# Dense products of three gated stages in three f32r passes, with the delta output's norms moved one stage on

## What is computed

```python
z = h @ w_in[l]                       # split into the inputs of four mixers
o_a = hgrn2_mixer(a_q, a_f, a_i, a_g, lower_bounds[l], hgrn_norm_g[l])
o_b = gla_mixer(b_q, b_k, b_v, b_code, b_g, gla_w_gk2[l], gla_b_gk[l], gla_norm_g[l])
o_c = mla_mixer(c_q, c_kv, c_kr, ...)
o_d = gdn_mixer(d_q, d_k, d_v, d_beta, d_a, d_z, ...)     # gated delta rule
mix = concatenate([o_a, o_b, o_c, o_d]) @ w_out[l]
x = x + rms_norm(mix, post_mix_g[l])
```

## Time and profile before

| | us |
|---|---|
| median of 3 runs | 2296.11 (2295.84 to 2297.59) |
| the profiled execution, its own time | 2292.07 |
| its span in the profile | 2290.3 |
| PE busy | 2169.8 |
| DVE busy | 1208.1 |
| ACT busy | 898.2 |
| POOL busy | 45.6 |

### The profile page before, as it was taken

How to read it: one execution, slowest core, us unless ns; L and a number is a source line. 1 busy time by engine, 2 the same in 40 slices (tenths; PEclk the granted TensorE clock), 3 DMA queues, 4 the chain that set the end, 5 groups by cost and what they waited for, 6 DMA issues and landing times. The chain is left out here.

```text
span 2290.3 us, 35396 instructions
## 1 busy us (share of the span) xinstructions
PE 2169.8 (95%) x14540; PEld 1555.1 (68%) x14540; DVE 1208.1 (53%) x2075; ACT 898.2 (39%) x1611; POOL 45.6 (2%) x36
## 2 busy tenths in 40 slices
PE   7999999899999999989998999998999988999998
PEld 5784454588888777744446888886877566887546
DVE  5553344676662285543546666524537774444554
ACT  5423234433333354233344333333346553323462
POOL 2000001000000020000010000000000000000000
PEclk9999999999999999999999999999999999999999
DMA  5201110122222221011112222222221102222001
GB/s 199 74 3 46 48 55 32 63 92 97 106 92 92 92 74 56 22 38 56 38 38 80 104 92 92 102 82 97 97 90 56 38 19 92 93 92 85 26 1 37
DMA packets 23920, 159.79 MB, mean 70 GB/s; under 512 B 3024, under 2 KB 3664, under 8 KB 4944
## 3 DMA queue, kind: packets, MB, share of 16 engines
q1 hardware_dynamic: 23760, 157.53, 19.3%
HBM read 155.43 MB, written 2.10 MB: 69 GB/s over the span
## 5 line engine op out<-in xcount | busy, mean ns | idle before, releaser
L673 DVE TENSOR_TENSOR arena_r<-ring,arena_r 128x512 fp32r<-128x512 f32 x448 | 313.1, 706 | 453.7 <-ACT arena_r L664 450.9
L664 ACT ACTIVATE arena_r<-ring 128x512 fp32r<-128x512 f32 x448 | 278.3, 629 | 597.8 <-PE banks L714 566.4
L712 PE MATMUL banks<-oT_r,arena_r 128*128 128x512 f32 x1104 | 449.5, 407 | 13.0 <-DVE arena_r L673 9.0
L714 PE MATMUL banks<-oT_r,arena_r 128*128 128x512 f32 x1104 | 432.4, 392 | 0.0
L713 PE MATMUL banks<-hT_r,arena_r 128*128 128x512 f32 x928 | 363.6, 392 | 0.0
L713 PE MATMUL banks<-arena_r,arena_r 128*128 128x512 f32 x704 | 276.3, 392 | 0.0
L712 PEld LDWEIGHTS banks<-oT_r,arena_r 128*128 128x128 f32 x1104 | 208.8, 189 | 71.4 <-DVE arena_r L944 11.8
L712 PE MATMUL banks<-arena_r,arena_r 128*128 128x512 f32 x592 | 240.3, 406 | 15.2 <-DVE arena_r L704 10.9
L714 PEld LDWEIGHTS banks<-oT_r,arena_r 128*128 128x128 f32 x1104 | 208.5, 189 | 44.5
L714 PE MATMUL banks<-arena_r,arena_r 128*128 128x512 f32 x592 | 232.6, 393 | 0.0
L713 PEld LDWEIGHTS banks<-hT_r,arena_r 128*128 128x128 f32 x928 | 175.8, 189 | 41.6 <-issue 7.2
(11 more groups left out here) (387 smaller groups left out, 2927.7 us busy)
## 6 DMA issues: line engine op xcount, KB each, us to landing
ring<-weights SPq DMA_DIRECT2D x142, 1024.0 KB, 4.7
xT<-x_features SPq DMA_DIRECT2D x2, 1024.0 KB, 6.2
arena<-memory SPq DMA_DIRECT2D x2, 1024.0 KB, 4.9
y_features<-xT SPq DMA_DIRECT2D x8, 256.0 KB, 2.0
const<-constants SPq DMA_DIRECT2D x1, 1088.0 KB, 15.7
const<-constants SPq DMA_DIRECT2D x1, 512.0 KB, 16.4
arena<-positions SPq DMA_DIRECT2D x1, 256.0 KB, 2.7
small<-small_vectors SPq DMA_DIRECT2D x2, 68.5 KB, 6.4
```

The source lines that it names most:

```text
L664: act.activation(hi, self.stream.block(b, n), ACT.Copy).then_inc(self.chip.sem("hi_ready"), 1)
L673: vec.tensor_tensor(lo[:, 0:n * P], self.stream.block(b, n), hi[:, 0:n * P].bitcast(F32), ALU.subtract).then_inc(self.chip.sem("lo_ready"), 1)
L712: pe.matmul(out, w_hi, hi, start=k == 0, stop=False)
L714: ins = pe.matmul(out, w_lo, hi, start=False, stop=k == nk - 1)
```

## The change

1. In `Meanwhile.steps`, units from `first_split` on are made by `split_product_steps`, three f32r passes a block, instead of `product_steps`. `GLA_WHOLE = (1, 0, 2)` units of each gated stage stay whole: of 32, 40 and 32 blocks 24, 40 and 24 are split, 88 a layer, 176 in two layers.
2. ScalarE and VectorE make the parts. First gated stage: eight row tiles of `chip.h` and six weight chunks of four blocks. The second uses the same row parts and makes ten chunks. The third: four row tiles (`chip.o` 0, 1, 6, 7) and six chunks. ScalarE's copies of rows and of the first chunks stand before the copy of the log decays into `LF_HI`, which is now line 1770 and signals `silu_ready`.
3. The norms of the delta output leave the delta stage. Its squares and gate products stay there; the two norm matmuls, the Ln and Exp and the two products come in the first gated stage, late (`left = 2`).
4. The blocks between the steps are given by a table, `GLA_RUNS`.
5. SP's loads in these stages wait for low parts of the ring's slot and for the whole units (`whole`). Of five empty blocks in the weights' layout three move ahead of `outad`, so its chunks start on a multiple of four.

```diff
     def steps(self, pe):
         for u in range(self.u0, self.u1):
-            for k in product_steps(self.chip, pe, self.stream, u, self.rhs):
+            if u < self.first_split:
+                walk = product_steps(self.chip, pe, self.stream, u, self.rhs)
+            else:
+                made = (lambda k: pe.wait_ge(self.chip.sem("x_lo"), k + 1)) if u == self.first_split and self.rhs else None
+                walk = split_product_steps(self.chip, pe, self.split, u, self.parts, each=made)
+            for k in walk:
...
-            meanwhile.tensor(pe, blocks=4)
-            pe.wait_ge(chip.sem("sq_ready"), 2)
-            for h in range(2):
-                made(pe.matmul(fill(f"out{h}"), chip.c("blk64"), SQ[h], start=True, stop=True))
             meanwhile.tensor(pe)
...
-            act.preload_act_table_set(EXP_LN)
-            for h in range(2):
-                rstd_of(f"out{h}", RN[h], 64.0)
             meanwhile.scalar(act)
...
-            for h in range(2):
-                vec.wait_ge(chip.sem("rstd_ready"), 5 + h)
-                v(tt(chip.o(6 + h), OG[h], RN[h], ALU.mult))
...
+GLA_RUNS = ((3, 5, 2, 2, 3, 2, 1, 3, 1, 4, 1, 2),
+            (4, 5, 3, 2, 4, 3, 1, 4, 2, 4, 2, 2),
+            (1, 3, 2, 1, 4, 3, 1, 3, 1, 3, 3, 3, 1, 1, 1))
+GLA_WHOLE = (1, 0, 2)
...
+    if group == 0:
+        first, more = [(46, 47), (48, 12), (5, 6), (7, 8), (9, 10), (AI, AQS)], []
+        early = 2
+    elif group == 1:
+        first, more = [(13, 14), (15, 16)], [(5, 6), (7, 8), (46, 47), (48, 12), (AQ, AQS), (AK, AI)]
+        early = 9
+    else:
+        parts = lambda k: (chip.t_r(41 + k), chip.t_r(45 + k))
+        first, more = [(33, 34), (35, 36), (37, 38), (12, 49), (50, 51), (52, 53)], []
+        early = 4
...
-            meanwhile.tensor(pe, blocks=3)
+            dense()
...
+                for h in range(left):
+                    pe.matmul(chip.T.fill(pe), chip.c("blk64"), D_SQ[h], start=True, stop=True).then_inc(chip.sem("t_ready"), 1)
...
+            if group != 1 and split:
+                for i in range(KD if hgrn else 4):
+                    hi_part(chip, act, i, source(i), parts(i)[0])
+            if group == 0:
+                split.scalar_chunks(act, 2)
+            if group == 1:
+                split.scalar_chunks(act, 10)
+            if group == 2:
+                if split:
+                    split.scalar_chunks(act, 2)
                 meanwhile.scalar(act, 1)
-            act.activation(LF_HI, chip.T.full(act, LFT), ACT.Copy).then_inc(chip.sem("hi_ready"), 1)
-            if not hgrn:
+                if split:
+                    split.scalar_chunks(act, 6)
+            act.activation(LF_HI, chip.T.full(act, LFT), ACT.Copy).then_inc(chip.sem("silu_ready"), 1)
...
+            for h in range(left):
+                act.activation(D_R[h], chip.T.full(act, DELTA + h), ACT.Ln, bias=chip.c("eps"), scale=1.0 / 64.0).then_inc(chip.sem("t_used"), 1)
+                act.wait_ge(chip.sem("t_used"), DELTA + h + 1)
+                act.activation(D_R[h], D_R[h], ACT.Exp, scale=-0.5).then_inc(chip.sem("rstd_ready"), 1)
...
+            if group != 1 and split:
+                for i in range(apart):
+                    lo_part(chip, vec, i, source(i), *parts(i))
+            if split:
+                split.vector_chunks(vec, early)
+            vec.wait_ge(chip.sem("silu_ready"), 1)
             tt(LF_LO, chip.T.full(vec, LFT), LF_HI.bitcast(F32), ALU.subtract).then_inc(chip.sem("t_used"), 1)
...
+            for h in range(left):
+                vec.wait_ge(chip.sem("rstd_ready"), h + 1)
+                v(tt(chip.o(6 + h), D_OUT[h], D_R[h], ALU.mult))
```

96 lines of the change are left out of this document (67 added, 29 removed).

## The result

The changed kernel takes **2278.94 us** (median of 4 runs, 2276.88 to 2283.4); the kernel before, in the same session, 2296.85 (4 runs, 2295.84 to 2298.98). The ratio is 0.9923, with a 95% interval of 0.9906 to 0.9941: 17.9 us less. The forecast was 2274.5 (2262 to 2287), so sign and range held and the time came 4.4 us above it.

The account below looks back on a forecast made before the run. TensorE, busy 95% of the span, was taken as the bound. Terms of -4.8, -4.1, -4.0 and +2.1 gave -10.8 us a layer, -21.6 in two: 2270.5 profiled, 2274.5 as median, range 2262 to 2287.

Parts of the forecast that it names:

- End of the delta stage, -4.8: Delta stage's end: with the norms gone, ScalarE's last evacuation follows the last block; next stage starts 4.8 us earlier a layer.
- First gated stage, -4.1: 24 split blocks save 4.4 us, norm matmuls cost 1.7, steady clock saves 1.7, waits cost 0.3: -4.1 a layer.
- Second gated stage, -4.0: 40 split blocks save 7.3 us, less 1.6 at the start, 0.9 at the end, 0.8 for clock: -4.0 a layer.
- +0.8 for the clock: Second gated stage: idle time at its start may drop the clock; half of 1.7 us counted as cost.
- the ScalarE tail: Second gated stage's end: norm, then three evacuations with a table load between end 2.0 us after the last product, not 1.2: +0.9.
- The 1.6 of the first chunk: Second gated stage's start: TensorE waits for VectorE's first split weight chunk, beginning at 2.0 us instead of 0.46: +1.6.
- Third gated stage, +2.1: 24 split blocks save 4.4 us of work, but waits for decays and selects, late evacuations and a clock drop give +2.1 a layer.
- the offset: Whole kernel: the median lies 4.0 us above the profiled execution, taking the forecast from 2270.5 to 2274.5.
- all covered: Rival, gated stages: all extra copies fit in idle time and no clock drops; about -20.5 us a layer, 2255; chance 0.13.
- copies in the chain: Rival, gated stages: 6 to 10 more copies a layer exposed, costing 4 to 6 us; 2283 to 2291; chance 0.14.
- clock flapping: Rival, gated stages: repeated clock drops at 1.7 us each, 13 more to undo the gain, 17 give 2303; chance 0.05.
- the half rate: Rival, split blocks: an fp32 block is worth only two passes, so 176 split blocks add 40 us, 2336; chance 0.01.

Follow-up runs that it names:

- e1: Kernel before with only the delta output's norms moved into the first gated stage, all gated products whole fp32: 2282.09 us, ratio 0.9946.
- e5: Changed kernel with nearly all new copies left out, passes and order kept, so gated dense products differ from the reference's: 2271.23 us, ratio 0.9901.
- e10: e8 with the second gated stage's gate unit emptied early, logarithm table loaded there, last two operations swapped, one filler fewer: 2264.33 us, ratio 0.9872.
- e6: Changed kernel with VectorE's first low part ahead of the three gate instructions in the second gated stage: 2277.42 us, ratio 0.9925.
- e4: Changed kernel plus unread filler products: one at the second gated stage's start, two each at the second's and third's ends: 2275.24 us, ratio 0.9904.
- e7: Changed kernel with the early decay copy of e3 and the border fillers of e4 together: 2264.61 us, ratio 0.9872.
- e8: Changed kernel with the third gated stage whole and the fillers of e4, but one at the third stage's end: 2263.11 us, ratio 0.9860.
- e3: Changed kernel with the third stage's log decay copy ahead of an evacuation and four weight chunks, two low parts ahead, not four: 2275.65 us, ratio 0.9916.
- e2: Changed kernel with the third gated stage whole as before, the first two still split: 2270.99 us, ratio 0.9898.
- e9: Kernel before with norms moved, all three gated stages whole, one filler at the second's end and one at the third's: 2274.80 us, ratio 0.9918.

## Why the prediction was right, and where not

**End of the delta stage, -4.8: right, 4.6.** ScalarE at that place, after; its squares start at 186.41:

```profile
186.41 1.09 ACT L1389 ACTIVATE arena<-banks 128x512 f32<-128x512 f32 x2 [11.99 <-PE banks L1327]
188.31 0.60 ACT L767 ACTIVATE arena<-banks 128x512 f32<-128x512 f32 x1 [0.81 <-PE banks L751]
189.37 1.28 ACT L1740 ACT_TABLE_LOAD   x1 [0.47 <-PEq L1131]
```

From the squares to the next stage's table load it was 7.53 us and is 2.96. The evacuation follows the last block, as worked out. The border took 0.46 us behind the last end, not 0.31, hence 4.6. The whole stage is 4.0 us shorter in the first layer and 1.7 in the second of the profiled execution, 4.5 and 4.7 in e1's; where the rest went is not shown.

**First gated stage, -4.1: direction and mechanism right, size 3.3.** The clock at its start stays up (1.00, for the 0.56 of the earlier trace rows), the two norm matmuls cost 1.7 (e1), the copies 0.4 (e5; put at 0.3). Mis-sized was the price of a split block in place. I took 0.18 us off per block from 90 passes in a row, but here passes come in runs of 3 to 12 between small matmuls. After, and then e1 with three fp32 blocks in one run:

```profile
211.90 0.50 PE L715 MATMUL banks<-arena_r,arena_r 128*128 128x512 f32 x1
212.24 0.40 PE L716 MATMUL banks<-arena_r,arena_r 128*128 128x512 f32 x1
212.48 0.40 PE L717 MATMUL banks<-arena_r,arena_r 128*128 128x512 f32 x1
...
213.87 0.39 PE L717 MATMUL banks<-arena_r,arena_r 128*128 128x512 f32 x1
214.19 1.16 PE L1628 MATMUL banks<-arena 64*64 64x64 f32 x64
```

```profile
218.22 2.84 PE L751 MATMUL banks<-hT,ring 128*128 128x512 f32 x6
221.00 1.15 PE L1716 MATMUL banks<-arena 128*64 128x64 f32 x32
```

A run of three split blocks lasts 214.19 - 211.90 = 2.29 us, one of three fp32 blocks 221.00 - 218.22 = 2.78. That is 0.163 a block, 3.9 for 24; less the 0.4 of e5 it is 3.5, and e1 against after gives 3.3. Both runs carry some 0.2 us beyond their steps (2.78 is 6 x 0.43 and 0.2; 2.29 is 9 x 0.233 and 0.2), so the slow first pass of 0.34 us is not what is lost. It is that the passes stand 0.233 us apart here (212.24 to 213.87, seven steps), for 0.227 in the long run. Why they do stays open.

**Second gated stage, -4.0: the mechanism right, the size smaller.** My -4.0 held +0.8 for the clock, so at the upper clock it stood for -4.8; measured are 4.1 there, and 3.4 as the mean of the two layers. 40 x 0.163 = 6.5 for the 7.3 put; the first pass starts at 232.43, 2.0 us after the start as predicted (+1.6); the ScalarE tail was put at 0.9, and e10, which takes it away, gains 0.8. 6.5 - 1.6 - 0.8 = 4.1. The clock fell in it in one layer of two, as the half chance said, and cost 1.3. The 1.6 of the first chunk is a real term, but not one that an earlier low part gives back: in e6 the next chunk's wait took its place.

**Third gated stage, +2.1: the sign right, the size 1.8, the parts partly luck.** Most of what I counted was there: the copy of the decays starts 12.3 us after the stage (put at 10.9), TensorE idles before the decays, ScalarE waits before it for 0.80 us for VectorE, as in the kernel before, and, which I had not counted, for 1.54 us for the first whole product, at the lower clock, the wait for the selects is 1.31 (put at 1.7), and the two evacuations stand behind the norms (the idle time before the latent stage is 2.67, for 1.21 before). I put the idle time before the decays at 3 to 4 us with a clock drop behind it. The changed kernel shows 1.91 and no drop there, because the drop came earlier: the stage begins after 2.29 us of idle time, 1.43 before, and runs at the lower clock from 2.1 us to 9.0 us after its start. e4 and e6, which began it at the upper clock, show 3.52, within my 3 to 4, and the drop. What I had not seen is how little this stage can use of less work on TensorE: 1.9 of 4.1 us with hardly any copies (e5), nothing with them (e7 against e8).

**Latent stage, nothing: +1.6, and the cause is open.** I stopped at the stages that the change touches. The clock is what makes it longer: 0.95 before and 0.92 after, in both layers. The idle time ahead of it has grown from 1.21 to 2.67 us with the change, and a drop follows within 2.5 us of the stage's start in all eight stages that begin after such an idle time (after, e3, e5, e6). But behind 1.21 us it follows too, in four of six, and e1 and e2, which have that idle time, show three latent stages of 66.5 and 66.6. So it is not shown that the wider border costs the 1.6.

**The sum.** I forecast -10.8 a layer. By the windows of the first layer it is -4.0 - 3.3 - 2.8 + 1.8 + 1.6, which is -6.6 before rounding, in the profiled execution, by those of the second -5.7 (its delta stage gave only 1.7, at PEclk 0.96 for 0.98), together the 12.4 of the span; what the rest of the program gained and lost cancels. And the offset was wrong: I took the profiled execution as 4.0 below its kernel's median for both kernels, but after's lies 0.8 above. So a forecast of 2270.5 for the profiled execution was 9.2 off, and the one for the median 4.4; the agreement of the medians is partly that second error.

It is luck in another way too. My terms gave 9.6 us to the norms and 12 to the splits. By the medians the norms gave 13.8 (e1, 9.4 to 15.2; its stages account for 9, the rest goes with the clock) and the splits of all three stages only 3.1 more, or 5 by the ratios, since the third stage and the clock took back what the first two gained: where the third stage is whole and the borders are filled, the splits of the first two alone are worth 11.7 (e9 to e8).

Of the rivals, "all covered" fell with the 1.91 us of waiting before the decays and the 2.0 at the second stage's start, "copies in the chain" is true of the third stage alone (e5), clock flapping did occur, in single drops, 13 us more at the lower clock in the whole span, far from the 13 drops it needed, and the half rate is excluded by the first stage's gain of 3.3 us, an argument that rests on the rows alone. (Its 2336 also left out what the norms give.) The Trainium skill's page "Perfetto Trace Analysis", section "Engine Utilization", halves the rate for FP32_LOW_HIGH; by that, as I used it, the stage would have got longer, and the measurement decides against it.

What stays open: why a third stage or a latent stage of the same kernel gets its drop in one layer and not in the other (e2, e7, e10 all show it) can't be told from these runs, and so single runs of one kernel spread by 3 to 10 us.

## What to carry to other kernels

Before taking work off the busiest engine, ask how far its work can shrink before a chain through the other engines becomes the limit, and whether what buys the smaller work stands in that chain: here a stage in which TensorE is busy over 95% of the time gave nothing back for 3 us less of its work, and 1.9 of 4.1 us when the copies for it were left out. Take the granted clock of each window into every comparison, also one stage further than the edit reaches. A few products that nobody reads, put where TensorE idles anyway, gained about 7 us where the third stage's splits gained none. Measure the parts of a change apart, since a total that agrees can hide one part that gave more and one that gave less. And price an instruction among the work it will stand in, not in the longest run of the trace.

## What was not expected of the hardware

The granted clock fell after idle times as short as 1.2 to 2.7 us, and never where fillers left less than 1 us. This counts the stage starts of all twelve profiled executions, and how many have a stretch at the lower clock that begins between 1.1 us before and 2.6 us after:

| start of | TensorE's idle time | runs | with a drop |
|---|---|---|---|
| first gated stage | 3.98 | before | 2 of 2 |
| first gated stage | 1.14 | all others | 0 of 22 |
| third gated stage | 2.29 | after, e2, e3, e5, e6 | 6 of 10 |
| third gated stage | 1.43 | before, e1 | 3 of 4 |
| third gated stage | 0.57 | e4, e7 to e10 | 0 of 10 |
| latent stage | 2.67 | after, e3, e5, e6 | 8 of 8 |
| latent stage | 1.21 | before, e1, e2 | 4 of 6 |
| latent stage | 0.57 or 0.96 | e4, e7 to e10 | 0 of 10 |

One pair of traces would not show this. The kernel after has 0.50 near the start of its third stage:

```profile
279.72:286.55 6.83, 6.83 (x40) 2.86 (x39) 6.11 (x11) 5.34 (x10) 0.00 (x0) 0.50 0.00 0
```

That is TensorE busy without a gap at half its clock. But e6 begins the same stage behind the same idle time and without a filler, and stays up:

```profile
274.69 1.09 PE L751 MATMUL banks<-arena,ring 16*128 16x512 f32 x2 [2.29 <-PEq L1607]
```

```profile
274.64:283.20 8.56, 8.51 (x58) 4.18 (x58) 5.77 (x10) 7.70 (x14) 0.00 (x0) 1.00 0.00 0
```

The Trainium skill's page "TensorE: Matmul & The Clock Gate", section "What's actually happening", says that the gate follows how busy TensorE has been recently, and the rows with fillers agree (0 of 20 for 21 of 28 at the same two starts without them). Fillers changed the median by 7.3 us with all products whole (e1 to e9, 2282.09 to 2274.80) and by 7.9 with the third stage whole (e2 to e8, 2270.99 to 2263.11), in both cases with intervals that do not overlap, and by 3.7, no more than the noise, in the changed kernel, where the third stage's queue gave the gain back (e4).
